# A one-core program of three transformer blocks, last stage a mixture of experts: an earlier signal for the first expert round, and sums added up in the output tensor

## The chip, the cores and the metric

The kernel runs on one core of one Trainium2 chip. The metric is the device time of one execution in microseconds. The median of 3 runs of the kernel before is 1987.92 us (1987.85 to 1988.99).

## The reference

Three blocks follow each other on x of 256 tokens by 1024 features, all in fp32: attention with an mLSTM, adaptive attention with a feed-forward part, and a third block of two layers with memory attention. The change touches only the last step, the mixture of experts of the third block:

```python
def moe_swiglu(h, router, we_gate, we_up, we_down):
    logits = (h @ router)
    top_v, top_i = lax.top_k(logits, 2)
    top_w = jax.nn.softmax(top_v, axis=-1)
    gates = sum(one_hot(top_i, 8) * top_w[..., None], axis=-2)
    for e in range(8):
        out = out + gates[..., e:e+1] * ((silu(h @ we_gate[e]) * (h @ we_up[e])) @ we_down[e])
x = x + moe_swiglu(rms_norm(x), ...)          # the output
```

Each expert has three weight matrices of 1024 x 3584 numbers, 44 MB in fp32. Each token goes to two of the eight experts, so there are 512 pairs of a token and an expert.

## The kernel before, in words

**Rounds.** The expert stage runs in rounds, one per expert (more if an expert has over 96 tokens; in the profiled execution there are 8). A round has 96 slots for tokens (CAP), handled as 3 tiles of 32 (TILES). 8 rounds have 768 slots for 512 pairs; the slots left over are empty.

**Memory tensors.** Three tensors in the chip's memory serve the rounds. `hrows` holds the 256 normalized token rows, `xrows` the 256 rows of the residual, to which the experts' results are added; both have 128 spare rows behind them. `slot_rows` says for every slot of every round which token row it holds and with what gate. A slot that nobody fills names one of the spare rows, number 256 or above. A row is cut into four quarters of 256 numbers (1 KB), one quarter per group of 32 partitions, so row r has the indices 4r to 4r + 3.

**TensorE (PE).** `expert_round` (L1651 and on) does gate half 0, gate half 1, up half 0, up half 1 (L1665), then down (L1682). At its top it waits for `rows_turned`: the round's tokens, transposed, stand in `hg`. For the first round `hg` comes another way, since no round before it fetched the rows: PE multiplies the token rows with a selection matrix `Pm` (`gather_first`, L1639), and ScalarE (ACT) copies the result to `hg` in two halves (L1736). PE waits for both copies, and then for `rows_turned` "first".

**VectorE (DVE).** After the router it ranks the experts (L3183 and on), builds `Pm` (L3198), copies the counts out of the bank (L3204), sums up the gates (L3207), works out rounds, slots and entries (L3208 to L3263), then waits in `name_rows("first")` (L3268, L3269) for the first table of rows, and after it gives `rows_turned` "first" with a copy of one column (L3274). In each round it takes the gates (L3278), names the next round's rows, multiplies gate and up (L3287), transposes (L3288), and transposes the next round's tokens into `hg`. The gate of the next round is taken once the last scatter of this one has landed.

**GpSimd (POOL).** It stores spare entries, spare rows (L3368), `xrows` (L3369) and `hrows` (L3371), waits until all have landed, stores the entries (L3386), loads the first table (L3380) and enters the rounds. In each: three scatters with an add in the transfer put the results `ey` of the round before into `xrows` (L3397; in the first round the addresses are spare rows), then the table and the three gathers of the next round's tokens from `hrows` (L3404). After the last round three more scatters follow (L3410).

**SyncE (SP).** It streams the weights in pieces of 1 MB and 0.75 MB through 16 buffers (the 7 of `ring`, `x_even`, the 8 of `x_odd`), 48 pieces per round (L659). A piece is issued when PE has used up the buffer 16 pieces earlier (L646). Two neighbouring pieces share a semaphore, and PE waits for both. When the last scatters have landed SP copies `xrows` to the output (L676), waits for that and ends.

Of the kernel before, what the change touches and what calls it, by code (L numbers as in the profile page):

```python
# [30 lines left out]
F32 = mybir.dt.float32  # L31
F32R = mybir.dt.float32r
I32 = mybir.dt.int32
ALU = mybir.AluOpType
ACT = mybir.ActivationFunctionType
AX = mybir.AxisListType.X

P = 128
S = 256
NT = S // P  # L40
D = 1024
# [249 lines left out]
def program(nc, A, out, const_at, known=None, upto=9):  # L291

    c = Count(known[0] if known else None)
# [3 lines left out]
    with ctx:  # L297
# [5 lines left out]
        def sb(name, *shape, dt=F32):  # L303
            return ctx.enter_context(nc.sbuf_tensor(name, [P, *shape], dt))
# [9 lines left out]
        ident, ones = C("ident"), C("ones")  # L314
# [3 lines left out]
        xres = sb("xres", NT, D)  # L318
# [26 lines left out]
        rt = sb("rt", 6, NT, NEXP)  # L345
        cmp = sb("cmp", 2, NT * 64)
        pos = sb("pos", 3, NT, NROUND + 1)
        xtr = sb("xtr", 8, 8)
# [3 lines left out]
        with ExitStack() as phase:  # L352
# [8 lines left out]
            junk = sa("junk", D)  # L361
# [38 lines left out]
        with ExitStack() as phase:  # L400
# [6 lines left out]
            ey, hg = sm("ey", TILES, 256), sm("hg", KC, CAP)  # L407
            Pm, rows_q = sm("Pm", NT, CAP), sm("rows_q", TILES, 256)
            gate_of, target = sm("gate_of", TILES), sm("target", TILES)
            targeti, nexti = sm("targeti", TILES, dt=I32), sm("nexti", TILES, dt=I32)  # L410
# [5 lines left out]
        hparts = [junk[:, 0:512], nrm[:, 0, 0:512], junk[:, 512:1024], nrm[:, 0, 512:1024]]  # L416
        relrow = nc.dram_tensor("relrow", (P, HEADS1, 511), F32, kind="Internal").ap()
        hrows = nc.dram_tensor("hrows", (S + P, D), F32, kind="Internal").ap()
        xrows = nc.dram_tensor("xrows", (S + P, D), F32, kind="Internal").ap()
        slot_rows = nc.dram_tensor("slot_rows", ((NROUND + 1) * CAP, 2), F32, kind="Internal").ap()  # L420

        def xslot(i):
# [93 lines left out]
        for g, group in enumerate(vgroups):  # L516
            r, loads = 0, []
            for name, n in group:
# [5 lines left out]
                else:  # L524
                    first = 96 if g == 3 else 0
# [20 lines left out]
        def _(sp):  # L546
# [76 lines left out]
            if upto >= 4:  # L623
                v = A["sw_w_in_3"][0].rearrange("(k p) n -> p k n", p=P)
# [11 lines left out]
            if upto >= 5:  # L636
                W.first = W.n
                gate, up = (A[f"sw_we_{x}_3"].rearrange("a e (p k) n -> (a e) p k n", p=P) for x in ("gate", "up"))
                down = A["sw_we_down_3"].rearrange("a e f n -> (a e) f n")

                def expert(e):

                    for j, (name, k) in enumerate(ROUND_PIECES):
                        i, half = j % XSLOTS, int(name[-1])
                        for q in range(4):
                            sp.wait_ge(*(c.at(f"x_used{q}", j - XSLOTS) if j >= XSLOTS else c.before(f"x_used{q}", j + len(ROUND_PIECES) - XSLOTS)))  # L646
                        if j < RING:
                            name_, v = W.known.freed[W.first + j - RING] if W.known else ("piece_used", 1)
                            sp.wait_ge(c.sem(name_), v)
                        elif j < XSLOTS:  # L650
                            sp.wait_ge(*J.full("aO", SW_PAIRS + SM_PAIRS - 1))
                            if j == XSLOTS - 1:
                                sp.wait_ge(*c.at("piece_used", "so", 3))
                        if name[:4] == "down":
                            f0 = half * XWIDE[0]
                            src = down[e, f0:f0 + XWIDE[half], :].rearrange("(p r) n -> p (r n)", p=P)[:, k * XWIDE[half]:(k + 1) * XWIDE[half]]
                        else:
                            src = (gate if name[:4] == "gate" else up)[e, :, k, half * XWIDE[0]:half * XWIDE[0] + XWIDE[half]]
                        sp.dma_start(xslot(i)[:, 0:XWIDE[half]], src).then_inc(c.sem(xlanded(i)[0]), 16)  # L659

                with sp.Fori(0, NEXP) as r:
                    c.loop = r
                    expert(r)
                    c.loop = None

                sp.wait_ge(*c.at("rounds_ready"))
                n_rounds = sp.value_load(ridi[0:1, 15:16], min_val=NEXP, max_val=NROUND)
                with sp.If(n_rounds > NEXP):
                    with sp.Fori(NEXP, n_rounds) as r:
                        e = sp.value_load(ridi[0:1, bass.ds(r, 1)], min_val=0, max_val=NEXP - 1)  # L670
                        c.loop = r
                        expert(e)
                        c.loop = None

                sp.wait_ge(c.sem("last_added"), 16 * TILES)
                sp.dma_start(out.rearrange("a s d -> (a s) d"), xrows[0:S, :]).then_inc(c.sem("out_stored"), 16)  # L676
                sp.wait_ge(c.sem("out_stored"), 16)
                return
            for h in range(2):
                for t in range(NT):  # L680
# [1639 lines left out]
        def _(dve):  # L2320
            v = nc.vector

            def do(ins, s=None):

                s = s or c.sig("vec_step")
                ins.then_inc(s.sem, 1)
                dve.wait_ge(s.sem, s.val)
# [191 lines left out]
            for t in range(NT):  # L2519
                r = invert("pre", t)  # L2520
# [96 lines left out]
            for i in range(MH + 1):  # L2617
                if i < MH:
                    x = logit[:, i % 4, 0:384]
# [10 lines left out]
                    for t, col, nk in T384:  # L2630
                        x = logit[:, i % 4, col:col + nk * P]
# [8 lines left out]
                if i >= 1:  # L2640
# [4 lines left out]
                    for t in range(NT):  # L2645
                        x = nrm[:, t, h * MD:(h + 1) * MD]
# [7 lines left out]
            for h in range(MH):  # L2654
                for t in range(NT):
                    x, j = nrm[:, t, h * MD:(h + 1) * MD], 2 * (NT * h + t)
# [33 lines left out]
            for i in range(HEADS1 + 3):  # L2690
# [11 lines left out]
                if i >= 3:  # L2702
                    h = i - 3
                    dve.wait_ge(*J.emptied("b1p", 12 + h // 2))
                    x = mix1[:, h, :]
# [180 lines left out]
            for p, (name, g) in enumerate(FFN["ff"]):  # L2886
                low(2 * p + SPLITS + 1)
                if name == "ff1":
                    x = add_main(ffa["ff"][:, g % 2, :], "ff1", g)
# [172 lines left out]
            for q in range(KC // 2):  # L3062
                dve.wait_ge(*c.at("h_high", "cvf", q))
                for j in range(2):
                    k = 2 * q + j
                    s = c.sig("h_split", "cvf", k)
# [3 lines left out]
            for p, (name, g) in enumerate(FFN["dn"]):  # L3070
                low(2 * p + SPLITS + 1)
                x = ffa["dn"][:, g % 2, :]
# [57 lines left out]
            for i in range(SW_PAIRS + SM_PAIRS + 3):  # L3130
# [22 lines left out]
                for p in (0, 1) if i == 1 else (i - 1,) if 3 <= i <= SW_PAIRS + SM_PAIRS else ():  # L3153
# [5 lines left out]
                    for j in range(2):  # L3159
                        for t, col, nk in T384 if p < SW_PAIRS else T512:  # L3160
                            x = slog[:, (2 * p + j) % 6, col:col + nk * P]
# [42 lines left out]
            do(v.tensor_copy(count, b[:, 16:24]), J.free("slots"))  # L3204
            dve.wait_ge(*c.at("exp_done", "router"))
            do(v.tensor_tensor(flat(rt[:, 4, :, :]), flat(rt[:, 2, :, :]), flat(rt[:, 1, :, :]), ALU.mult))
            do(v.tensor_reduce(xtr[:, 0:NT, 1], rt[:, 4, :, :], AX, ALU.add))  # L3207
            do(v.reciprocal(xtr[:, 0:NT, 2], xtr[:, 0:NT, 1]))  # L3208
            do(v.tensor_tensor(pos[:, 2, :, 0:NEXP], rt[:, 4, :, :], spread(xtr[:, 0:NT, 2], 8), ALU.mult))

# [28 lines left out]
            at_r, here, place, first = (room[:, x * 2 * NROUND:(x + 1) * 2 * NROUND].rearrange("p (t r) -> p t r", t=NT) for x in range(4))  # L3239
# [31 lines left out]
            name_rows("first")  # L3271
            wide_banks = (ps[0], ps[1], ps[2]), (ps[3], acc[0], acc[1])
            n_rounds = dve.value_load(ridi[0:1, 15:16], min_val=NEXP, max_val=NROUND)
            do(v.tensor_copy(xtr[:, 6, 3:4], ones[:, 0:1]), c.sig("rows_turned", "first"))  # L3274
            with dve.Fori(0, n_rounds) as r:
                c.enter(r)
                dve.wait_ge(*c.at("rows_added", TILES - 1))
# [3 lines left out]
                for half in range(2):  # L3281
                    n = XWIDE[half] // 4
# [16 lines left out]
        def _(pool):  # L3299
            g = nc.gpsimd  # L3300

            def do(ins, s=None):
                s = s or c.sig("pool_step")
                ins.then_inc(s.sem, 1)
                pool.wait_ge(s.sem, s.val)
# [13 lines left out]

                return bass.AP(tensor=ap.tensor, offset=ap.offset, ap=[ap.ap[0], [0, 4], ap.ap[1]])  # L3320

            xquads = xrows.rearrange("r (q n) -> (r q) n", q=4)
            pool.wait_ge(*c.at("exponent"))
            pool.wait_ge(*c.at("moments"))
            pool.dma_start(gm, everywhere(A["ada_b_2"][:, 2 * D:3 * D], D)).then_inc(c.sem("gates_bias_in"), 16)
# [25 lines left out]
            for x in range(2):  # L3351
                for y in range(2):
                    rows = slice(H64 * y, H64 * (y + 1))
# [10 lines left out]
            spare = C("spare")  # L3364
            do(g.tensor_copy(spares[:, :, 1], bass.AP(tensor=spare.tensor, offset=spare.offset, ap=[spare.ap[0], [0, NROUND + 1]])))
            pool.dma_start(slot_rows.rearrange("(r s) n -> s r n", s=CAP), spares[0:CAP, :, :]).then_inc(c.sem("rows_stored"), 16)
            for rows in (hrows, xrows):
                pool.dma_start(rows[S:S + P, :], junk[:, :]).then_inc(c.sem("rows_stored"), 16)  # L3368
            pool.dma_start(xrows[0:S, :].rearrange("(t p) d -> p t d", p=P), xres[:, :, :]).then_inc(c.sig("rows_added", "first", by=16).sem, 16)  # L3369
            pool.wait_ge(*c.at("gained"))  # L3370
            pool.dma_start(hrows[0:S, :].rearrange("(t p) d -> p t d", p=P), nrm[:, :, :]).then_inc(c.sem("rows_stored"), 16)  # L3371
            pool.wait_ge(c.sem("rows_stored"), 64)
            pool.wait_ge(*c.at("rows_added", "first"))
            hquads = hrows.rearrange("r (q n) -> (r q) n", q=4)
            by_round = slot_rows.rearrange("(r x t) n -> r t x n", r=NROUND + 1, x=TILES)
# [16 lines left out]
            with pool.Fori(0, n_rounds) as r:  # L3392
                c.enter(r)
                pool.wait_ge(*c.at("ey_ready"))
                pool.sem_inc(c.sem("sums_asked"), 1)
                for x in range(TILES):
                    g.indirect_dma_start(xquads, bass.IndirectOffsetOnAxis(ap=targeti[:, x:x + 1], axis=0), ey[:, x, :], None, compute_op=ALU.add)\  # L3397
                        .then_inc(c.sig("rows_added", x, by=16).sem, 16)
                pool.wait_ge(*c.at("targets_set"))
                load_rows(bass.ds(r + 1, 1), "next")  # L3400
                pool.wait_ge(*c.at("rows_named", "next"))
                pool.sem_inc(c.sem("rows_asked"), 1)
                for x in range(TILES):
                    g.indirect_dma_start(rows_q[:, x, :], None, hquads, bass.IndirectOffsetOnAxis(ap=nexti[:, x:x + 1], axis=0))\  # L3404
                        .then_inc(c.sig("rows_in", x, by=16).sem, 16)
                c.leave()
            c.loop = None
            for x in range(TILES):
                pool.wait_ge(*c.at("ey_last", x))
                g.indirect_dma_start(xquads, bass.IndirectOffsetOnAxis(ap=targeti[:, x:x + 1], axis=0), ey[:, x, :], None, compute_op=ALU.add)\  # L3410
                    .then_inc(c.sem("last_added"), 16)
        del block
    return c, J, W
# [36 lines left out]
```

## Time and profile before

| | us |
|---|---|
| median of 3 runs | 1987.92 |
| profiled execution, its own time | 1988.2 |
| its span (first to last instruction) | 1986.5 |
| PE busy | 1912.8 |
| DVE / ACT / POOL busy | 861.9 / 544.2 / 121.8 |
| expert rounds, from PE's first to last of them | 1101.5 to 1971.6 |
| mean granted TensorE clock | 0.986 |

Busy times are sums over the whole span. The granted clock is in shares of the full TensorE clock: 1.00 is 2.4 GHz and 0.50 is 1.2 GHz. "DMA share" is the mean busy share of the core's 16 DMA engines.

### The profile page before, as it was taken

To read this page: it belongs to the slowest core of one execution; us is meant where nothing else is said; L and a number is where in the kernel's file an instruction comes from. 1 tells how busy PE (TensorE), PEld (TensorE's weight loads), DVE (VectorE), ACT (ScalarE), POOL (GpSimd) and SP (SyncE) were. 2 spreads that over 40 slices of the span, in tenths; PEclk is the share of its full clock that TensorE was granted. 3 is DMA by queue.
4 is the path that set the end of the run, shared out by engine and by line. 5 is a ranking of instruction groups with operands and counts; after the bars stand their busy time and mean duration, and the time that the engine had idled before them with its cause. 6 is when DMAs were issued, how large, how long until landed. Compare 5 with 4: busy or idle time off the path is not lost.

```text
span 1986.5 us, 41226 instructions
## 1 busy us (share of the span) xinstructions
PE 1912.8 (96%) x17136; PEld 1243.0 (63%) x17136; DVE 861.9 (43%) x1564; ACT 544.2 (27%) x959; POOL 121.8 (6%) x139
## 2 busy tenths in 40 slices
PE   8999999999999999999995899999999999999996
PEld 7786889758888888888854244443535353444434
DVE  6577786787776986666554020201101020202011
ACT  2331356554444575545552000000000000000000
POOL 0000000000000000000201201001010202020100
PEclk9999999999999999999997899999999999999999
DMA  9788754346553416555227799999999999999993
GB/s 310 162 317 300 265 183 153 106 149 209 172 193 107 147 44 214 189 190 149 96 85 254 275 416 399 416 408 414 412 411 416 405 418 401 418 406 417 406 416 132
DMA packets 184301, 545.32 MB, mean 275 GB/s; under 512 B 32028, under 2 KB 87221, under 8 KB 159285
## 3 DMA queue, kind: packets, MB, share of 16 engines
q1 hardware_dynamic: 170877, 525.32, 69.5%
q0 software_dynamic: 8048, 13.03, 2.6%
q10 hardware_dynamic: 5208, 4.49, 1.3%
q8 instruction: 135, 2.21, 0.5%
q14 instruction: 33, 0.27, 0.0%
HBM read 534.00 MB, written 9.84 MB: 274 GB/s over the span
## 4 chain that ended last, share of the span: by engine, by line
PE 91%; DVE 4%; DMA 2%; ACT 1%; issue 1%; POOL 1%; SPq 0%; POOLq 0%; DVEq 0%; ACTq 0%
PE bank L1665 21%; PE sum L1682 15%; PE sum L1665 8%; PE bank L1275 7%; PE sum L1257 7%; PE bank L759 5%; PE bank L1277 4%; PE sum L823 2%; PE bank L924 2%; PE bank L777 1%; DMA hrows<-nrm 1%; PE sum L1347 1%; PE sum L803 1%; PE sum L804 1%; PE sum L805 1%
## 5 line engine op out<-in xcount | busy, mean ns | idle before, releaser
L1665 PE MATMUL bank<-ring,hg 128*32 128x512 f32 x2688 | 293.8, 596 | 26.4 <-DVE xtr L3274 26.4
L1665 PEld LDWEIGHTS bank<-ring,hg 128*32 128x32 f32 x2688 | 91.1, 111 | 220.9 <-issue 220.0
L1275 PE MATMUL bank<-hT_hl,w_hi 128*128 128x512 f32 x608 | 216.5, 399 | 2.0 <-DVE hT_hl L2465 1.3
L2488 DVE TENSOR_TENSOR w_lo<-ring,w_hi 128x1024 fp32r<-128x1024 f32 x130 | 156.0, 1223 | 77.5 <-ACT w_hi L2042 76.5
L1665 PE MATMUL sum<-x_odd,hg 128*32 128x384 f32 x2048 | 189.3, 486 | 0.0
L2042 ACT ACTIVATE w_hi<-ring 128x1024 fp32r<-128x1024 f32 x130 | 136.8, 1060 | 125.5 <-PE sum L1257 66.3
L1277 PE MATMUL bank<-hT_hl,w_lo 128*128 128x256 f32 x608 | 170.7, 281 | 0.0
L3287 DVE TENSOR_TENSOR gated<-gated,bank 128x512 f32<-128x512 f32 (+1 forms) x32 | 20.9, 655 | 340.1 <-PE bank L1665 259.9
L2302 ACT ACTIVATE ey<-sum,gate_of 128x256 f32<-128x256 f32 x24 | 11.4, 474 | 501.6 <-PE sum L1682 497.2
L1682 PE MATMUL sum<-ring,actT 128*32 128x256 f32 x2688 | 146.5, 379 | 0.0
L3278 DVE COPY gate_of<-row_table 128x3 f32<-128x3 f32 x8 | 1.4, 170 | 332.6 <-DMA xrows<-ey,targeti 332.6
L1275 PEld LDWEIGHTS bank<-hT_hl,w_hi 128*128 128x128 f32 x608 | 114.2, 188 | 31.7 <-DVE hT_hl L2465 1.8
L1665 PEld LDWEIGHTS sum<-x_odd,hg 128*32 128x32 f32 x2048 | 69.1, 110 | 96.0 <-issue 96.0
L1682 PE MATMUL sum<-x_odd,actT 128*32 128x256 f32 x2304 | 125.8, 379 | 0.0
L1682 PEld LDWEIGHTS sum<-ring,actT 128*32 128x32 f32 x2688 | 90.7, 110 | 56.0 <-issue 3.0
L1277 PEld LDWEIGHTS bank<-hT_hl,w_lo 128*128 128x128 f32 x608 | 114.8, 189 | 0.9
L1682 PEld LDWEIGHTS sum<-x_odd,actT 128*32 128x32 f32 x2304 | 77.8, 110 | 46.6
L1665 PE MATMUL bank<-x_odd,hg 128*32 128x384 f32 x1024 | 106.7, 486 | 0.0
L759 PE MATMUL bank<-hT,ring 128*128 128x256 f32 x448 | 100.8, 386 | 2.5 <-DMA ring<-in_w_in 1.8
L759 PEld LDWEIGHTS bank<-hT,ring 128*128 128x128 f32 x448 | 86.4, 194 | 16.8 <-issue 4.9
L2308 ACT ACTIVATE gated<-bank 128x512 f32<-128x512 f32 (+1 forms) x32 | 18.2, 570 | 283.3 <-PE bank L1665 173.8
L3397 POOL DMA_INDIRECT xrows<-ey,targeti x24 | 38.2, 1592 | 582.4 <-ACT ey L2302 576.7
(643 smaller groups left out, 2995.1 us busy)
## 6 DMA issues: line engine op xcount, KB each, us to landing
ring<-in_sw_we_gate SPq DMA_DIRECT2D x56, 1024.0 KB, 9.4
ring<-in_sw_we_up SPq DMA_DIRECT2D x56, 1024.0 KB, 10.3
ring<-in_sw_we_down SPq DMA_DIRECT2D x56, 1024.0 KB, 10.6
x_odd<-in_sw_we_gate SPq DMA_DIRECT2D x64, 768.0 KB, 8.1
x_odd<-in_sw_we_up SPq DMA_DIRECT2D x64, 768.0 KB, 10.7
x_odd<-in_sw_we_down SPq DMA_DIRECT2D x64, 768.0 KB, 9.7
ring<-in_w_in SPq DMA_DIRECT2D x36, 1024.0 KB, 9.0
ring<-in_w_ff SPq DMA_DIRECT2D x32, 1024.0 KB, 5.5
```

Source lines behind the costliest of these rows:

```text
L759: last = mm(ps[b][:, j * S:(j + 1) * S], w[k][:, c0 + j * P:c0 + (j + 1) * P], hT[:, k, :], start=(k == 0), stop=(k == KC - 1))
L823: last = mm(acc[2 * t + h][:, :], mixT[:, 2 * k + j, t * P:(t + 1) * P], w[:, j, h * 512:(h + 1) * 512], start=(k == first and j == 0), st ...
L924: mm(ps[banks[q]][:, j * S:(j + 1) * S], w[k][:, q * S + j * P:q * S + (j + 1) * P], hT[:, k, :], start=(k == 4 and j == 0), stop=False)
L1257: last = mm(acc[2 * t + h][:, :], a[:, g % 4, tok], w[:, h * 512:(h + 1) * 512], start=(g + half + x == 0), stop=False)
L1275: mm(o[:, :].rearrange("p (a n) -> p a n", a=2), hi[:, k, cols], hT_hl[:, :, kk, :], start=(kk == 0), stop=False)
L1277: last = mm(o[:, 0:S], lo[:, k, cols], hT_hi[:, kk, :], start=False, stop=(kk == KC - 1))
L1665: last = mm(wide_banks[half][x][32 * q:32 * q + 32, 0:n], hg[:, k, 32 * x:32 * x + 32], w[:, n * q:n * (q + 1)], start=(k == 0), stop=(k = ...
L1682: last = mm(o, actT[half][:, x, n * p + i, :], w[piece][:, at_:at_ + 256], start=(half + p + i == 0 and x != 1), stop=(half == 1 and p == ...
L2042: go(f(w_hi[:, hp % SPLITS, :], ring[:, W.place(key), lo:lo + PIECE // 2], ACT.Copy), c.sig("ff_hi", stage, hp))
L2488: v.tensor_tensor(w_lo[:, hp % SPLITS, :], ring[:, W.place(key), lo:lo + PIECE // 2], w_hi[:, hp % SPLITS, :].bitcast(F32), ALU.subtract). ...
L3287: do(v.tensor_tensor(gated[half][:, x, :], gated[half][:, x, :], wide_banks[half][x][:, 0:n], ALU.mult))
L3397: g.indirect_dma_start(xquads, bass.IndirectOffsetOnAxis(ap=targeti[:, x:x + 1], axis=0), ey[:, x, :], None, compute_op=ALU.add)\
```

## The change

First, VectorE gives `rows_turned` "first" with the instruction that sums the gates, right behind the copy that empties the bank of the slots; the copy of one column behind `name_rows("first")` is gone. Second, the tensor `xrows` is gone: the residual is stored in the output tensor, the scatters add to it there, and SP's copy at the end and its wait are gone. The output has no spare rows, so the scatters get a bound: an index above 4 x 256 - 1 is skipped without an error. Third, the store of spare rows into `xrows` is gone with it, and POOL waits for 48 on that semaphore instead of 64.

```diff
-        xrows = nc.dram_tensor("xrows", (S + P, D), F32, kind="Internal").ap()
...
                 sp.wait_ge(c.sem("last_added"), 16 * TILES)
-                sp.dma_start(out.rearrange("a s d -> (a s) d"), xrows[0:S, :]).then_inc(c.sem("out_stored"), 16)
-                sp.wait_ge(c.sem("out_stored"), 16)
                 return
...
-            do(v.tensor_reduce(xtr[:, 0:NT, 1], rt[:, 4, :, :], AX, ALU.add))
+            do(v.tensor_reduce(xtr[:, 0:NT, 1], rt[:, 4, :, :], AX, ALU.add), c.sig("rows_turned", "first"))
...
             n_rounds = dve.value_load(ridi[0:1, 15:16], min_val=NEXP, max_val=NROUND)
-            do(v.tensor_copy(xtr[:, 6, 3:4], ones[:, 0:1]), c.sig("rows_turned", "first"))
...
-            xquads = xrows.rearrange("r (q n) -> (r q) n", q=4)
+            xquads = out.rearrange("a s (q n) -> (a s q) n", q=4)
...
-            for rows in (hrows, xrows):
-                pool.dma_start(rows[S:S + P, :], junk[:, :]).then_inc(c.sem("rows_stored"), 16)
-            pool.dma_start(xrows[0:S, :].rearrange("(t p) d -> p t d", p=P), xres[:, :, :]).then_inc(c.sig("rows_added", "first", by=16).sem, 16)
+            pool.dma_start(hrows[S:S + P, :], junk[:, :]).then_inc(c.sem("rows_stored"), 16)
+            pool.dma_start(out.rearrange("a (t p) d -> p (a t) d", p=P), xres[:, :, :]).then_inc(c.sig("rows_added", "first", by=16).sem, 16)
...
-            pool.wait_ge(c.sem("rows_stored"), 64)
+            pool.wait_ge(c.sem("rows_stored"), 48)
...      (both scatters, in the rounds and behind them)
-                    g.indirect_dma_start(xquads, bass.IndirectOffsetOnAxis(ap=targeti[:, x:x + 1], axis=0), ey[:, x, :], None, compute_op=ALU.add)\
+                    g.indirect_dma_start(xquads, bass.IndirectOffsetOnAxis(ap=targeti[:, x:x + 1], axis=0), ey[:, x, :], None, bounds_check=4 * S - 1, oob_is_err=False, compute_op=ALU.add)\
```

## Rows read from the trace of the kernel before

**Rows 1.** What PE waited for at line 1665, whole span: us, times.

```profile
  DVE xtr L3274: 26.4, 1
```

**Rows 2.** Chain that ended last, 1060 to 1102 us: start, us, what.

```profile
1061.51 26.25 DMA hrows<-nrm
...
1092.04 3.49 DMA slot_rows<-entry,placei
...
1097.54 1.85 DMA row_table<-slot_rows
...
1101.08 0.17 DVE xtr L3274
1101.25 0.25 issue
1101.50 1.03 PE bank L1665
```

**Rows 3.** Timeline, 1060 to 1125 us: start, us, engine, line, what, count, [idle before, releaser].

```profile
1067.52 0.17 DVE L3207 TENSOR_REDUCE xtr<-rt 128x2 f32<-128x16 f32 x1
...
1075.18 0.49 ACT L1736 ACTIVATE hg<-bank 128x384 f32<-128x384 f32 x1 [3.32 <-PE bank L1639]
...
1081.92 1.49 ACT L2302 ACTIVATE ey<-sum,gate_of 128x256 f32<-128x256 f32 x3 [3.91 <-DMA xrows<-xres]
...
1102.88 1.56 POOL L3397 DMA_INDIRECT xrows<-ey,targeti  x1 [0.30 <-issue]
...
1113.26 0.17 DVE L3269 CAST nexti<-target 128x3 int32<-128x3 f32 x1
```

**Rows 4.** Windows: stretch, its us, busy of PE, PEld, DVE, ACT, POOL (instructions), clock, DMA share, GB/s.

```profile
1072.00:1074.00 2.00, 2.00 (x10) 2.00 (x9) 1.76 (x8) 0.00 (x0) 0.00 (x0) 0.50 0.99 408
...
1082.00:1086.00 4.00, 0.00 (x0) 0.00 (x0) 0.00 (x0) 1.34 (x3) 0.00 (x0) 0.50 1.01 418
1086.00:1088.00 2.00, 0.00 (x0) 0.00 (x0) 0.00 (x0) 0.00 (x0) 0.00 (x0) 0.50 0.21 84
1088.00:1100.00 12.00, 0.00 (x0) 0.00 (x0) 0.47 (x2) 0.00 (x0) 7.32 (x9) 0.50 0.02 1
1102.00:1104.00 2.00, 2.00 (x12) 0.45 (x8) 0.00 (x0) 0.00 (x0) 1.70 (x2) 0.50 0.57 72
1106.00:1108.00 2.00, 2.00 (x20) 0.54 (x16) 0.34 (x2) 0.00 (x0) 0.19 (x1) 0.90 0.24 33
```

**Rows 5.** Windows of the first and the fourth round (columns as before).

```profile
1101.50:1140.20 38.70, 38.70 (x388) 13.61 (x392) 0.74 (x4) 1.79 (x3) 7.93 (x9) 0.94 0.91 330
1140.20:1176.30 36.10, 36.10 (x389) 12.96 (x385) 5.22 (x6) 1.47 (x3) 0.00 (x0) 1.00 1.01 417
...
1429.37:1537.79 108.42, 108.42 (x1444) 48.60 (x1440) 12.23 (x19) 4.68 (x9) 10.07 (x10) 1.00 1.02 412
```

**Rows 6.** Weight pieces, issue to landing: x_odd at 1059 to 1061; ring in rounds 1, 8.

```profile
DMA to landing us min/median/max: 26.3/27.3/28.3
...
DMA to landing us min/median/max: 5.0/7.9/8.5
...
DMA to landing us min/median/max: 9.6/10.5/23.1
```

**Rows 7.** One ring piece of down, round 8; first chain piece of down there.

```profile
L659 SPq DMA_DIRECT2D ring<-in_sw_we_down x1: 875/875/875, 1904.5 to 1904.5; - x1
...
DMA to landing us min/median/max: 23.1/23.1/23.1
...
1935.21 36.38 PE sum L1682 x672
```

**Rows 8.** POOL's groups, 1210 to 1980 us: busy, mean ns, idle before, releasers.

```profile
L3397 POOL DMA_INDIRECT xrows<-ey,targeti x21 | 33.4, 1589 | 580.9 <-ACT ey L2302 576.7 <-issue 4.3
L3404 POOL DMA_INDIRECT rows_q<-hrows,nexti x21 | 20.8, 992 | 50.5 <-DVE nexti L3269 46.3 <-issue 4.3
```

**Rows 9.** DMA issues, whole span: KB, median us to landing.

```profile
row_table<-slot_rows POOLq DMA_DIRECT2D x36, 0.8 KB, 5.3
...
xrows<-junk POOLq DMA_DIRECT2D x1, 512.0 KB, 15.6
xrows<-ey,targeti POOLq DMA_INDIRECT x27, 9.3
rows_q<-hrows,nexti POOLq DMA_INDIRECT x24, 6.7
```

**Rows 10.** The end of the program: chain and SP's timeline; issues after 1970 us.

```profile
1976.43 1.55 POOL xrows L3410
...
1980.24 0.62 SPq L676 DMA_DIRECT2D out_dram<-xrows  x1
...
xrows<-ey,targeti POOLq DMA_INDIRECT x3, 3.8
out_dram<-xrows SPq DMA_DIRECT2D x1, 5.8
```

More of the change, by code:

```diff
@@ L3409, in _ @@
                 pool.wait_ge(*c.at("ey_last", x))
-                g.indirect_dma_start(xquads, bass.IndirectOffsetOnAxis(ap=targeti[:, x:x + 1], axis=0), ey[:, x, :], None, compute_op=ALU.add)\
+                g.indirect_dma_start(xquads, bass.IndirectOffsetOnAxis(ap=targeti[:, x:x + 1], axis=0), ey[:, x, :], None, bounds_check=4 * S - 1, oob_is_err=False, compute_op=ALU.add)\
                     .then_inc(c.sem("last_added"), 16)
```

## The prediction

> **What bounds the kernel now.** I read the page first: PE is busy 96% of the span, so most of the time is matmuls, and only what starts or ends that work, or a hole in it, can matter. Then the list of waits for line 1665, the first line of an expert round: there is one hole, 26.4 us, and what ended it is VectorE's one-column copy [rows 1]. The chain of that stretch says what that copy itself sat behind: the store of `hrows` took 26.25 us to land, then came the entries, the table of rows, and only then the signal [rows 2]. PE uses none of these in the first round. Its tokens come from `hg`, and the timeline has the second half of `hg` copied at 1075.18 + 0.49 = 1075.67 us [rows 3]. So PE could have begun there and began at 1101.50.
>
> Then the windows, to see what bounds the rounds themselves. A middle round is 108.42 us long and PE is busy for all 108.42, at clock 1.00, while the DMA engines' share is 1.02 and 412 GB/s move [rows 5]. Both are full. PE sets the pace as long as pieces land before PE wants them, and how near that is has to be read from the landings (below), since it decides whether an earlier start is kept to the end. Last the tail: last scatter issued at 1976.43, output copy at 1980.24, end of the span 1986.5 [rows 10].
>
> **The signal.** It moves to the sum at L3207, which ends at 1067.52 + 0.17 = 1067.69 [rows 3]. PE still waits for both copies of `hg`, so the later of the two decides: 1075.67. From the end of the old signalling copy (1101.25) to PE's first matmul the chain has 0.25 us [rows 2]; taking the same, PE starts at 1075.92. The gain is 1101.50 - 1075.92 = 25.6 us. The removed copy is 0.17 us on an engine that is idle most of a round: nothing.
>
> **The clock at the start.** In the old start PE ran at 0.50 until some point in 1106 to 1108, and gate halves 0 and 1 took 38.70 us where the same number of matmuls at full clock takes 36.10: 2.6 us lost [rows 4, 5]. The new start also finds the clock at 0.50, because it had fallen during the selection matmuls (2.00 of 2.00 us busy at 0.50 in 1072 to 1074 [rows 4]). If it rises at once, 2.6 us are gained; if it takes as much again as the old start, 2.6 are lost. I take the same loss as before: the rows show nothing to prefer. The Trainium skill, TensorE: Matmul & The Clock Gate, Part 1, says that the slow clock is the default state and that activity releases it. By that rule the selection matmuls, which end just before, would help the clock rise sooner, and the sum would be up to 2.6 us lower. The trace speaks half against it: those matmuls ran busy for several us and the clock stayed at 0.50 [rows 4].
>
> **Who is late next in round 1.** ACT's first `ey` waits for the store of the residual, which lands by 1081.9 [rows 3]; then it needs PE's gate half 0, some 24 us into the round. No loss. VectorE is the one to check. Its row-naming chain does not move earlier, and now runs beside weight traffic. The old chain was done at 1113.26 + 0.17 = 1113.4 [rows 3]. Entries landed in 3.49 and the table in 1.85 us on quiet DMA engines [rows 2]; under load I give the entries the scatters' 9.3 and the table its median 5.3 [rows 9]: + 5.8 and + 3.5. The first scatter then also lands under load instead of quiet (3.7 to 3.8 us as in the tail [rows 10], against 9.3): + 5.5. Sum + 14.8, done at 1128.2. VectorE is wanted when up half 0 is done. Half 0 is 8 of a matrix's 14 MB, so 36.10 x 8/14 = 20.6 us [rows 5], and that is at 1075.9 + 38.7 + 20.6 = 1135.2. So 7 us are left there, and PE itself waits for VectorE only at the start of down, 1075.9 + 38.7 + 36.1 = 1150.7. Cost: nothing. Were the cover gone, each us that VectorE is later than that would be a us of PE's.
>
> **The weights' stream.** This is where a gain could be given back. Before, the 16 buffers were full at about 1086.5, the engines rested (share 0.02 in 1088 to 1100 [rows 4]), and new pieces were issued from some 5.5 us after PE's start. Landing then took 5.0 us and in round 1 at most 8.5; in round 8 the slowest take 23.1 while the median is 10.5 [rows 6]. So part of the DMA engines falls behind by about (23.1 - 8.5) / 7 = 2.1 us in each round, and the margin shrinks to: issued 1904.5, landed 1927.6, wanted 1935.2, that is 7.6 us [rows 7]. In the new kernel the first piece is issued at 1075.9 + 5.5 = 1081.4, when the last of the old ones still has until 1060.0 + 28.3 = 1088.3 [rows 6], less the 0.5 MB of spare rows that are no longer written (512 KB at 418 GB/s [rows 4]: 1.25 us), so 1087.0. The new piece queues for 5.6 us, about 2.5 of which the 5.0 us of a lone piece already hide (1 MB at 418 GB/s is 2.5 us, the other half is overhead that overlaps): the added lag is 3 to 5.6 us. Against it stands what the scatters save. 768 slots for 512 pairs leave a third empty, all in the first round. A round's scatters write 384 rows of 1 KB; the read and the write of a third of them is 0.26 MB, 0.6 us at 418 GB/s, in each of 7 rounds: 4.2 us less lag by the end if the slow engines get their share of it. The lag in round 8 comes to 23.1 + (3 to 5.6) - (0 to 4.2), 22 to 28.7 us, against 30.7 at which PE waits (23.1 + 7.6). PE keeps its pace. I take a cost of nothing, with up to 5 us if the lag grows faster than in the old trace.
>
> The Trainium skill, DMA: Bandwidth & Descriptors, Latency and other measured facts, has two of the sixteen engines usually slower than the rest in traces, with GpSimd's descriptor traffic as a guess at why. The split of landings into 10 and 23 us agrees. By that guess fewer scatter descriptors would slow the growth of the lag and the rival below would be less likely.
>
> **The scatters.** No row shows one with a bound. GpSimd takes 1.59 us for an adding scatter and 0.99 us for a gather [rows 8]. The comparison is work for each index, the skipped row saves its descriptor. Bounds: 0.6 us less each (as the gather) and 1.6 us more (twice as long). In rounds neither matters, since POOL idles 580.9 us before them [rows 8]. In the tail three stand on the path: - 1.8 to + 4.8. I take 0, as the adding scatter is the nearest row. That the sums go to another tensor in the same kind of memory I cost at nothing too.
>
> **The tail.** The last scatter is issued at 1976.43 and lands 3.8 later, at 1980.2; the copy, issued at 1980.24, lands 5.8 later, at 1986.0; 0.5 us follow to the end at 1986.5 [rows 10]. Without the copy the end is 1980.2 + 0.5 = 1980.7: 5.8 us gained.
>
> **Sum.** Against the profiled execution: 1988.2 - 25.6 - 5.8 = 1956.8 us. The median of the runs is 0.3 below that execution, so 1956.5 us, 1.6% less than before.
>
> **The rivals.**
> 1. The weights come late. For it: share 1.01 to 1.02 in every round and a slowest landing that grows. Against it: the sum above leaves 2 us or more. It bites in round 7 or 8 as holes before L1665 or L1682; at an end lag 5 us above my bound it costs about 3 to 5 us: 1961.
> 2. The bounded scatter is dear on GpSimd, by 1.6 us each: + 4.8 us in the tail, 1961.3. For it: a comparison and a branch for each index in a place where 128 indices take 1.59 us. Against: nothing in the trace.
> 3. The signal does nothing, because PE waits for something else that comes late too (the round's own registers, or a bank). Against: the chain shows nothing else between 1075.67 and 1101.25. Only the tail is gained: 1982.1.
> 4. Slower than before: skipping is handled slowly by GpSimd. The tail pays three times the excess, so it decides from 31.4 / 3 = 10.5 us per scatter more than 1.59. In rounds there is room for three of those: POOL's chain starts some 3 us into a round and is done well before its half. At 12 us more each: 1956.5 + 36 = 1992.5. For it: nothing but that no row has this form. Against: the same engine does gathers of the same 128 indices in 0.99 us.
>
> **How the numbers follow.** Forecast 0.76, with its own range 1953.5 (clock up at once, scatters as gathers in part) to 1959.5 (clock as much later, some lag). Rival 1: 0.11, rival 2: 0.07, rival 3: 0.02, rival 4: 0.03; 0.01 for what I don't see, which I put to no change. A measurement of this kernel tells apart about 0.2%, 4 us. Faster 0.96, same 0.01, slower 0.03. The range takes most of the first two rivals in: 1953.5 to 1961.5.
>
> **What would show it.** PE's first L1665 at about 1075.9, released by ACT's copy of `hg`. The clock's rise and the first two gate halves near 38.7 us. Rounds of 108.42 us without holes and a last matmul at about 1946. Slowest ring landings in the last round between 22 and 29 us. VectorE's naming of the next rows done by 1128 to 1136. No output copy, and three last scatters 1.6 us each. It is wrong if holes appear before L1665 late in the stage, if a scatter takes over 2 us, or if L1665 starts after 1080.

## The result, and the profile after

The changed kernel takes 1962.31 us in the median of 4 runs (1961.4 to 1963.85), against 1988.19 us for the kernel before (4 runs). The ratio is 0.987, 95% interval 0.9853 to 0.9887, so it is faster by 1.3%. The forecast was 1956.5 with a range up to 1961.5, so the gain is 26 us where 31.7 were expected. The profiled execution took 1961.4 us, with a span of 1959.7. Line numbers are 3 to 5 lower than before: the round's gate and up are L1662, down is L1679, the last scatters L3405.

The start went as forecast. The timeline of the changed kernel has VectorE's sum that now gives the signal, ACT's second copy of `hg` and PE's first matmul of a round:

```profile
1067.06 0.17 DVE L3204 TENSOR_REDUCE xtr<-rt 128x2 f32<-128x16 f32 x1
...
1074.71 0.49 ACT L1733 ACTIVATE hg<-bank 128x384 f32<-128x384 f32 x1 [3.32 <-PE bank L1636]
1075.30 19.86 PE L1662 MATMUL bank<-ring,hg 128*32 128x512 f32 x168 [0.69 <-issue]
```

PE begins 0.10 us behind ACT's copy, at 1075.30 instead of 1101.50: 26.2 us earlier, and in place of the wait of 26.4 us [rows 1] PE stands idle for 0.69. Of the 26.2, 0.47 come from everything ahead having run that much earlier in this execution (ACT's copy was at 1075.18 [rows 3]).

The windows (columns as in [rows 4]) show the clock and the rounds:

```profile
1076.00:1078.00 2.00, 2.00 (x16) 0.62 (x12) 1.69 (x10) 1.49 (x2) 0.00 (x0) 0.50 1.03 425
1078.00:1080.00 2.00, 2.00 (x24) 0.52 (x20) 0.21 (x2) 1.26 (x3) 0.00 (x0) 0.84 0.98 408
...
1075.30:1113.20 37.90, 37.90 (x388) 13.46 (x392) 2.88 (x16) 4.70 (x8) 11.15 (x11) 0.96 1.01 381
...
1402.40:1510.80 108.40, 108.40 (x1444) 48.72 (x1440) 12.24 (x19) 4.68 (x9) 10.06 (x10) 1.00 1.02 413
```

A mean of 0.84 over 2 us is 0.64 us at 0.50 and the rest at 1.00, so the clock rose at about 1078.6, 3.3 us after the first matmul; before it took 4.9 us (0.90 in 1106 to 1108 [rows 4]). The gate halves took 37.9 us instead of 38.7 [rows 5]. A middle round has PE busy for its whole length, as before. PE's last matmul ends at 1944.6 instead of 1971.6: 27.0 us earlier, of which 26.2 is the start and 0.8 the clock.

Then comes the end. After PE's last matmul the kernel before took 14.9 us (1971.6 to 1986.5), and the changed one takes 15.1 (1944.6 to 1959.7), though the copy of 5.8 us is gone. The timeline of the changed kernel, the closing instructions in the queues of GpSimd and SP (name, count, ns min/median/max, start) the landings of the last three scatters, and SP's waits (us, times, longest):

```profile
1944.87 1.49 ACT L2313 ACTIVATE ey<-sum,gate_of 128x256 f32<-128x256 f32 x3 [70.95 <-PE sum L1679]
1946.18 1.63 POOL L3405 DMA_INDIRECT out_dram<-ey,targeti  x1 [79.39 <-ACT ey L2313]
1948.12 1.59 POOL L3405 DMA_INDIRECT out_dram<-ey,targeti  x1 [0.30 <-issue]
1950.01 1.55 POOL L3405 DMA_INDIRECT out_dram<-ey,targeti  x1 [0.30 <-issue]
...
L297 POOLq DRAIN  x1: 12391/12391/12391, 1947.1 to 1947.1; - x1
L297 SPq DRAIN  x1: 13/13/13, 1952.9 to 1952.9; - x1
...
DMA to landing us min/median/max: 2.7/3.7/3.9
...
SPq L297 <- DMA out_dram<-ey,targeti: 39.5, 1, 39.5
SPq L297 <- PEq L297: 6.7, 1, 6.7
```

SP had its last landing by 1952.8, 2.8 us after the scatter's start where it was 3.8 before [rows 10], and was ready to end at 1952.9, as the forecast wanted. It then stood 6.7 us at the barrier that closes the block, the point at the end of the program where every engine waits for all the others. The row names PE's queue, but PE was done at 1944.6. The only engine not there is GpSimd: its closing DRAIN, the last instruction of its part of the program, stands in the queue from 1947.1, while the scatters still run, and ends 12.39 us later, at 1959.5. That is 7.9 us after its last scatter instruction ended (1950.01 + 1.55). The same two rows of the kernel before:

```profile
L297 POOLq DRAIN  x1: 12538/12538/12538, 1973.4 to 1973.4; - x1
...
L297 SPq DRAIN  x1: 13/13/13, 1986.2 to 1986.2; - x1
```

There the drain ended at 1986.0, also 8.0 us after the last scatter instruction, and SP, behind its copy, was there at 1986.2. The drain lay under the copy and ended 0.2 us ahead of it. It is in the trace of the kernel before, under L297, a line that the prediction did not read.

### The profile page after: what moved, and what is told of

It is laid out like the page before. It is cut to its first block, busy times and chain, and to the rows that moved or that the text cites. A ratio compares the mean times of both kernels' runs of the same rounds, so it can differ in the third digit from the quotient of the medians.

```text
span 1959.7 us, 41250 instructions
## 1 busy us (share of the span) xinstructions
PE 1911.6 (98%) x17136; PEld 1244.1 (63%) x17136; DVE 861.6 (44%) x1563; ACT 544.2 (28%) x959; POOL 121.3 (6%) x138
## 4 chain that ended last, share of the span: by engine, by line
PE 91%; DVE 5%; ACT 1%; DMA 1%; issue 1%; SPq 0%; POOLq 0%; POOL 0%; DVEq 0%; ACTq 0%
PE bank L1662 21%; PE sum L1679 15%; PE sum L1662 8%; PE bank L1272 7%; PE sum L1254 7%; PE bank L756 5%; PE bank L1274 4%; PE sum L820 2%; PE bank L921 2%; PE bank L774 1%; PE sum L1344 1%; PE sum L800 1%; PE sum L801 1%; PE sum L802 1%; DMA ring<-in_w_out 1%
## 5 line engine op out<-in xcount | busy, mean ns | idle before, releaser
L1662 PE MATMUL bank<-ring,hg 128*32 128x512 f32 x2688 | 293.1, 595 | 0.7 <-issue 0.7
L1662 PEld LDWEIGHTS bank<-ring,hg 128*32 128x32 f32 x2688 | 91.2, 111 | 194.4 <-issue 193.4
L1662 PE MATMUL sum<-x_odd,hg 128*32 128x384 f32 x2048 | 189.3, 486 | 0.0
L2039 ACT ACTIVATE w_hi<-ring 128x1024 fp32r<-128x1024 f32 x130 | 136.8, 1060 | 125.3 <-PE sum L1254 66.3
L1679 PE MATMUL sum<-ring,actT 128*32 128x256 f32 x2688 | 146.5, 379 | 0.0
L1662 PEld LDWEIGHTS sum<-x_odd,hg 128*32 128x32 f32 x2048 | 69.3, 110 | 95.8 <-issue 95.8
L1679 PEld LDWEIGHTS sum<-ring,actT 128*32 128x32 f32 x2688 | 91.0, 110 | 55.8 <-issue 3.0
L1679 PE MATMUL sum<-x_odd,actT 128*32 128x256 f32 x2304 | 125.8, 379 | 0.0
L1679 PEld LDWEIGHTS sum<-x_odd,actT 128*32 128x32 f32 x2304 | 78.0, 110 | 46.4
L1662 PE MATMUL bank<-x_odd,hg 128*32 128x384 f32 x1024 | 106.7, 486 | 0.0
L3392 POOL DMA_INDIRECT out_dram<-ey,targeti x24 | 38.2, 1592 | 550.9 <-ACT ey L2299 545.0
```

Of the source, the lines that this page charges most:

```text
L1662: last = mm(wide_banks[half][x][32 * q:32 * q + 32, 0:n], hg[:, k, 32 * x:32 * x + 32], w[:, n * q:n * (q + 1)], start=(k == 0), stop=(k = ...
L1679: last = mm(o, actT[half][:, x, n * p + i, :], w[piece][:, at_:at_ + 256], start=(half + p + i == 0 and x != 1), stop=(half == 1 and p == ...
L2039: go(f(w_hi[:, hp % SPLITS, :], ring[:, W.place(key), lo:lo + PIECE // 2], ACT.Copy), c.sig("ff_hi", stage, hp))
```

## The experiments

The theory after the result: the program ends at the later of two, the copy (where there is one) and GpSimd's drain, and the drain ends about 7.9 us behind the last scatter instruction. The rival: the bound, or adding in the output tensor, makes the end slow.

**e1, the signal alone.**

```diff
-            do(v.tensor_reduce(xtr[:, 0:NT, 1], rt[:, 4, :, :], AX, ALU.add))
+            do(v.tensor_reduce(xtr[:, 0:NT, 1], rt[:, 4, :, :], AX, ALU.add), c.sig("rows_turned", "first"))
...
-            do(v.tensor_copy(xtr[:, 6, 3:4], ones[:, 0:1]), c.sig("rows_turned", "first"))
```

> The kernel before with only the early signal: xrows, its spare rows and the output copy stay. Theory 'drain' (GpSimd's closing drain ends 7.9 us after its last scatter instruction, and the program ends at the later of the drain and the output copy): the whole gain of the change comes from here, so 1961.5 to 1963 us, the same as the changed kernel within 1 us. Rival 'bounded tail' (the bound or the output tensor makes the end of the changed kernel slow, and costs back what the removed copy gave): the copy is still there and costs 5.8, so the same time, but then the trace's drain would end well before the copy lands; theory 'drain' has the drain's end within 0.3 us of the copy's landing. On the weights' stream: scatters write all rows, so the slowest landing grows by 2.1 us a round from about 14 in round 1 to 28 or more in round 8; if a third fewer rows is what slowed the growth in the changed kernel (1.5 us a round). PE should still not stall (limit 30.7).

Measured 1963.32 us (1962.16 to 1964.58), 0.9872 of before (0.9857 to 0.9887). The signal alone gives what the whole change gives, 25.2 of 25.9 us. Its drain ended at 1949.1 + 12.54 = 1961.6 and the copy's landing let SP go at 1962.3, so the two lie up to 0.7 us apart, more than the 0.3 that I had written down, with the drain still the earlier. On the weights' stream, the views of this trace give no landings of the `ring` pieces, so the expected 28 us can't be read. What can be read is the waits of PE's weight loads (us, times, longest); in the expert rounds of the changed kernel none of them was for a transfer:

```profile
PEld bank L1665 <- DMA ring<-in_sw_we_up: 0.2, 1, 0.2
```

A piece in the last round came 0.2 us too late for a weight load; the matmuls hid it. That is the edge of rival 1, without a cost yet.

**e2, the output tensor alone**: the changed kernel with the first signal back in its old place (the two diff lines of e1 reversed).

> The changed kernel with the signal put back to its old place: only the output tensor, the bound and the missing copy. Theory 'drain': 1988.19 less 0.2 (the distance of the old drain's end to the copy's end), so 1987.5 to 1988.3, no change that can be measured. My prediction's tail term would give 5.8 less: 1982.4. Rival 'bounded tail': at or above 1988.2, with a drain that begins or ends later against the last scatter than before (over 7.9 us).

Measured 1985.81 us (1984.17 to 1987.82), 0.9986 (0.9977 to 0.9995). The tail's term of 5.8 is refuted, and so is the rival: the drain ended at 1972.3 + 12.39 = 1984.7, again 7.9 us behind the last scatter (1975.21 + 1.55). But 2.7 us is more than the 0.2 that the theory allows. GpSimd's wait for the store of `hrows`, from the timelines of the kernel before and then of e2:

```profile
1088.06 1.09 POOL L3386 DMA_INDIRECT slot_rows<-entry,placei  x1 [25.83 <-DMA hrows<-nrm]
```

```profile
1086.93 1.09 POOL L3382 DMA_INDIRECT slot_rows<-entry,placei  x1 [23.19 <-DMA hrows<-nrm]
```

The wait is 2.6 us shorter, and with the old signal PE stands behind it.

**e7, e2 with a store of 0.5 MB put back**, to a tensor of its own, in the place of the removed store:

```diff
+        xspare = nc.dram_tensor("xspare", (P, D), F32, kind="Internal").ap()
...
             pool.dma_start(hrows[S:S + P, :], junk[:, :]).then_inc(c.sem("rows_stored"), 16)
+            pool.dma_start(xspare[:, :], junk[:, :]).then_inc(c.sem("rows_stored"), 16)
...
-            pool.wait_ge(c.sem("rows_stored"), 48)
+            pool.wait_ge(c.sem("rows_stored"), 64)
```

> Output tensor and bound without the early signal, and with the store of 128 spare rows (0.5 MB) put back, to a tensor of its own. e2 was 2.7 us faster than before where 0.2 was expected. Theory S (the missing 0.5 MB makes the store of hrows land 2.6 us sooner, and with the old signal PE waits for that): back to 1988.3, within 0.5 us of before. Rival (the tail or the lighter scatters gave the 2.7): it stays at 1985.8.

Measured 1988.67 us, 1.0001 (0.9992 to 1.001), and GpSimd's wait is back:

```profile
1087.60 1.09 POOL L3384 DMA_INDIRECT slot_rows<-entry,placei  x1 [25.66 <-DMA hrows<-nrm]
```

So the 2.7 us of e2 are the removed store of spare rows, and the output tensor, the bound and the missing copy together give nothing. In the whole change these 2.7 give nothing either, since PE no longer waits there: 25.2 + 2.7 is 27.9, and the two together gave 25.9.

**e3, the changed kernel without GpSimd's drain.** The program waits for its transfers by semaphores, so it does not rely on the drain for them.

```diff
-        block = ctx.enter_context(nc.Block())
+        block = ctx.enter_context(nc.Block(no_gpsimd_drain=True))
```

> The changed kernel, with the block closed without GpSimd's drain (all transfers are waited for by semaphores). Theory 'drain': the end is set by the landing of the last scatter at about 1952.8 plus 0.5 us, so 6.3 us less than the changed kernel: 1956.0. Rival (the 6.7 us at the end are a wait for something else, such as write-backs of the added rows, that any closing barrier would wait for): the same as the changed kernel, 1962.3.

Measured 1956.49 us (1955.39 to 1957.18), 0.9839 (0.9825 to 0.9852). SP's wait at the barrier went from 6.7 us to 0.2:

```profile
SPq L297 <- DMA out_dram<-ey,targeti: 41.8, 1, 41.8
SPq L297 <- PEq L297: 0.2, 1, 0.2
```

The drain is the cause: without it the time is the forecast's, 5.8 us below the changed kernel. That the two agree to the digit is in part luck. From PE's last matmul (1946.1) to the end (1954.7) it is 8.6 us where the forecast has 14.9 - 5.8 = 9.1: the last scatter lands 1.0 us sooner than before and the first of the three starts 0.55 later (e8), neither of which I had.

**e4, the kernel before without the drain** (the same line).

> The kernel before, closed without GpSimd's drain. Theory 'drain': the drain lay beside the output copy and ended 0.2 us before it, so the time stays within 0.3 us: 1988.0. Rival (closing without the drain is cheaper by itself, apart from what it hides): several us less.

Measured 1988.63 us, 1.0 (0.9991 to 1.0009). Covered by the copy, the drain costs nothing.

**e9, e1 without the drain**, the fourth corner.

> The kernel before with the early signal alone (xrows and the output copy stay), closed without GpSimd's drain. Theory 'the copy was covered': with the drain gone the copy is on the path for its full 5.8 us less 0.56 for the move ahead of the bounded scatter, so this is 5.2 us or so above e3 (1956.5): 1961.5 to 1962.5, and within 1 us of the same kernel with the drain (1963.3). Rival (the drain slows the end in some other way, and the copy never cost 5.8): near e3, below 1959.

Measured 1964.24 us (1962.94 to 1965.47), 0.9871 (0.9855 to 0.9888). It is 0.9 above e1, within both kernels' spread, and 7.8 above e3, where 5.2 was expected. The profiled executions (1965.31 and 1956.46) divide the difference: the part ahead of the rounds ran 2.3 us later than e3's (PE's first round matmul at 1078.02 against 1075.74), which has nothing to do with the end, and from PE's last matmul to the end it is 15.0 us (1948.6 to 1963.6) against e3's 8.6. These 6.4 are the copy's 5.9, less the 0.55 for the move, and 1.0 that the expectation missed: with the bound and the output tensor the last scatter lands 2.7 to 2.8 us after its start (the change, e2, e3, e5, e7, e8), and in `xrows` 3.7 to 3.8 (before, e1, e9). Which of the two edits does that no run tells apart. The rival, below 1959, is out. The copy and the drain lie side by side: taking away either gives 1 us at most, taking away both gives 6.8 by the medians and 6.3 by the tails of the traces (14.9 in the kernel before, 8.6 in e3).

| early signal in all four | with drain | without drain |
|---|---|---|
| with the copy | 1963.3 (e1) | 1964.2 (e9) |
| without the copy | 1962.3 (the change) | 1956.5 (e3) |

**e5, when the drain begins.** GpSimd waits for the last landings before it leaves the block:

```diff
                     .then_inc(c.sem("last_added"), 16)
+            pool.wait_ge(c.sem("last_added"), 16 * TILES)
```

> The changed kernel; GpSimd waits for the landing of its last three scatters before it leaves the block, so its drain begins about 1 us after the last scatter instruction has ended and not in its queue before it. Theory A (the drain ends a fixed time after the last transfer has landed or been issued): the drain's end does not move, about 7.9 us behind the end of the last scatter instruction. Theory B (the drain needs a time of its own once it can start): its end moves back by the time from the end of the scatter instruction to the landing, 1.3 us or more, to 9.2 us behind, and the drain's record is about 6.5 to 8 us long.

One execution, 1963.58 us. The last scatter instruction ended at 1950.84 + 1.55 = 1952.4. The drain:

```profile
L297 POOLq DRAIN  x1: 7876/7876/7876, 1953.8 to 1953.8; - x1
```

It started 1.4 us behind the scatter and took 7.88 us by itself, to 1961.7, 9.3 behind. Theory B holds: it is not a wait for the transfers, which had landed; it is a time of its own that starts once GpSimd has nothing left to do before it. What GpSimd does in that time no row shows.

**e6, one last scatter instead of three.**

```diff
-            for x in range(TILES):
-                pool.wait_ge(*c.at("ey_last", x))
+            for x in range(1):
+                pool.wait_ge(*c.at("ey_last", TILES - 1))
...
-                sp.wait_ge(c.sem("last_added"), 16 * TILES)
+                sp.wait_ge(c.sem("last_added"), 16)
```

> The changed kernel with only one of the three last scatters (tile 0, issued when all three results are there): the last round's sums of two tiles are left out. If the drain's cost is fixed behind the last scatter: its end is again 7.9 us behind the end of the scatter instruction, the whole 3.8 us earlier or so. If it grows with the number of transfers or descriptors still in the ring: clearly less than 7.9, down to 2.6.

One execution, 1958.77 us, of a kernel that leaves two tiles' sums out of the output. The timeline and the drain:

```profile
1947.47 1.63 POOL L3405 DMA_INDIRECT out_dram<-ey,targeti  x1 [80.43 <-ACT ey L2313]
...
L297 POOLq DRAIN  x1: 9577/9577/9577, 1947.2 to 1947.2; - x1
```

The scatter instruction ends at 1949.1, the drain at 1956.8: 7.7 us behind with one scatter, 7.9 with three. The cost is all but fixed against the number of last scatters; that it might depend on all that GpSimd issued before them was not tested. The drain's end moved 2.7 us earlier, less than the 3.8 that I expected, since this scatter waits for the third result.

**e8, e3 with the bound in a register**, set once ahead of the rounds.

```diff
+            bound = nc.gpsimd.alloc_register("bound")
+            nc.gpsimd.reg_mov(bound, 4 * S - 1)
...      (both scatters, this argument alone)
-  bounds_check=4 * S - 1
+  bounds_check=bound
```

> The changed kernel without GpSimd's drain, as e3, and with the bound put in a register once, ahead of the rounds, instead of a move ahead of each scatter. In the traces the first of the last scatters begins 0.83 us after its result is there, against 0.27 without a bound. Theory (the move ahead of the scatter costs 0.56 us there): 0.5 us below e3, 1956.0. Rival (the bound itself costs it): the same as e3. A difference of 0.5 us is at the edge of what timing tells; the trace decides, by the distance from the end of ACT's first result to the first scatter.

Measured 1955.53 us (1953.91 to 1958.57), 0.9836 (0.9822 to 0.9849), the fastest kernel here; against e3 the difference of 1 us is not clear of the spread. The timelines tell it. e8, then e3:

```profile
1946.00 1.49 ACT L2313 ACTIVATE ey<-sum,gate_of 128x256 f32<-128x256 f32 x3 [70.95 <-PE sum L1679]
1946.76 1.64 POOL L3407 DMA_INDIRECT out_dram<-ey,targeti  x1 [77.82 <-ACT ey L2313]
```

```profile
1946.37 1.48 ACT L2313 ACTIVATE ey<-sum,gate_of 128x256 f32<-128x256 f32 x3 [70.95 <-PE sum L1679]
1947.68 1.64 POOL L3405 DMA_INDIRECT out_dram<-ey,targeti  x1 [78.77 <-ACT ey L2313]
```

From ACT's start to the first scatter it is 0.76 us in e8 and 1.31 in e3. The kernel before, without a bound, has 0.75 (1971.85 to 1972.60). So it is not the bound itself: the move ahead of a bounded scatter costs 0.55 us once, on the path, and a register set early takes it off. The moves stand in the changed kernel's trace, and e8's has none at the scatters:

```profile
L3405 POOLq MOVE  x3: 29/29/29, 1945.4 to 1946.5; - x3
```

The move's own time is 29 ns; what the rest of the 0.55 us is, no row shows.

## Why the prediction was wrong

- **The step that failed** is in "The tail": "Without the copy the end is 1980.2 + 0.5 = 1980.7: 5.8 us gained." It read the end as one chain, scatter, copy, end, and took the end as 0.5 us behind the last landing. A second chain of nearly the same length lay beside it, GpSimd's drain of 7.9 us, and it set the end as soon as the copy was gone: with the drain in place the copy's removal gave 1.0 us, within the spread (e1 against the change), and without the drain 6.4 in the traces (e9 against e3). Against the profiled executions: the tail was to shrink by 5.8 us and grew by 0.2, which is 6.0 over; the earlier part ahead (0.47), PE's start 0.10 instead of 0.25 us behind ACT's copy, and the first round's clock (0.8) take 1.4 off, and 1956.8 + 6.0 - 1.4 = 1961.4, the measured time. None of my rivals had it. Rival 2 gives nearly the same time, 1961.3, for a wrong reason: the scatters with a bound take 1.55 to 1.63 us as before.
- **The signal** was right: 25.6 forecast, 26.2 measured (25.7 without the 0.47), and e1 gives 25.2 by itself.
- **The clock** lay within its bounds: 0.8 us gained in this execution, where I took nothing, and nothing is right for the early start as such. The chain's first piece of the round, 200 matmuls, took 23.9, 23.1, 23.9 and 23.2 us in the four profiled executions that start it after the long wait (before, e2, e4, e7), and 23.1, 23.1, 22.8, 22.9, 23.1, 24.1 and 24.2 in the seven that start it right behind the selection matmuls (the change, e1, e8, e5, e6, e3, e9). The two groups overlap, so the 0.8 us are chance as far as these runs tell. I had also weighed a rule of the Trainium skill, TensorE: Matmul & The Clock Gate, Part 1, that activity releases the slow clock. The gain that I worked out from it, up to 2.6 us, is not there in any of the seven. In the trace of the change PE was busy for all of 1068 to 1074, and the clock fell in that time (0.60 in 1068 to 1070, then 0.50).
- **VectorE's naming** stayed covered. The changed kernel's timeline:

```profile
1106.74 0.17 DVE L3266 CAST nexti<-target 128x3 int32<-128x3 f32 x1
...
1114.31 0.17 DVE L3274 COPY gate_of<-row_table 128x3 f32<-128x3 f32 x1 [7.40 <-DMA out_dram<-ey,targeti]
...
1122.56 0.17 DVE L3266 CAST nexti<-target 128x3 int32<-128x3 f32 x1
...
1134.53 0.69 DVE L3283 TENSOR_TENSOR gated<-gated,bank 128x512 f32<-128x512 f32 x1 [11.79 <-PE bank L1662]
```

It was done at 1122.7 (forecast 1128.2) and then waited 11.8 us for PE.
- **The weights' stream** held, with the lag that was worked out. Landings of `ring` pieces in rounds 1 and 8 of the changed kernel, as in [rows 6]:

```profile
DMA to landing us min/median/max: 9.4/12.4/13.7
...
DMA to landing us min/median/max: 9.9/11.6/24.0
```

It starts 5.2 us higher than before (13.7 against 8.5, forecast 3 to 5.6) and ends at 24.0 (forecast 22 to 28.7), since it grows by (24.0 - 13.7) / 7 = 1.5 us a round instead of 2.1. My estimate for the skipped rows was 0.6 less. The other traces of kernels with the early signal and the bound that give landings agree: 11.9 to 23.4 in e5, 12.2 to 23.3 in e6 and 11.3 to 22.8 in e8, 1.6 us a round. e1, which skips none, came to the edge of a wait; that fits, but its lag itself was not measured, so that the skipped rows slow the growth is argued and not shown. The prediction took the split into landings at 10 and at 23 us as some DMA engines being slower, for which it named the Trainium skill, DMA: Bandwidth & Descriptors, Latency and other measured facts. The split is there again (median 11.6, slowest 24.0), but no view here gives landings by engine, so whether it is engines, and which, no run here shows.
- **The scatters** cost what I took, 1.59 us each. Two terms were put at nothing and are not: the move ahead of the first of the last three, 0.55 us, which delays the drain as well, and the last scatter's landing, 1.0 us sooner, which the drain hides. The first of the two is part of why the tail of the change is no shorter than before.
- **The spare rows' store** I had counted only against the lag, and at 1.25 us; the landing of `hrows` moved by 2.5 (e7 against e2). e2 and e7 show that it was worth 2.7 us where PE waits for `hrows`, and nothing in the whole change.

## What to carry to other kernels

Before you credit the removal of the last step on the path, list every engine's closing instructions with their starts and lengths and ask which would end second: here a chain that ended 0.2 us earlier took the place of the one removed. Where GpSimd issues transfers until the end and all of them are waited for by semaphores, closing the block without its drain is worth trying (here 5.8 us); where something else covers the drain, it is worth nothing. An early signal costs one argument, and it is found by asking which of the things that the waiting engine stands behind it really uses.

## What the runs showed of the hardware

- GpSimd's closing drain took 7.88 us by itself with all transfers landed before it began (e5). Where it stood in the queue before the last scatters had run, it ended 7.9 to 8.0 us behind the last scatter instruction with three of them and 7.7 with one (e6).
- An adding scatter with a bound took GpSimd 1.59 us, the same as without, though a third of the slots' rows are skipped over all rounds. The skipped rows save traffic and not issue time: GpSimd's DMA queue moved 1.44 MB less with the bound (13.03 MB before, 11.59 in e7), which is what the rows of the empty slots and of the first round's scatters come to. A bound given as a constant puts a move ahead of the scatter, 0.55 us where it stands behind a wait.
- Beside a saturated weight stream 0.5 MB more to store made another store on the same queue land later: 26.1 us after its issue in e7 against 23.6 in e2, 2.5 us, twice what its bytes take at 418 GB/s.
